# A hybrid decoder layer on one core: 384 instead of 256 tokens gathered, the choice of experts in two stages

## The reference

```python
def peer_ffn(xn, wq, k1, k2, u_tab, v_tab):       # 16384 experts, 8 heads, top 16 a head
    q = (xb @ wq).reshape(P_BLOCK, P_HEADS, 2, half)
    v1, i1 = lax.top_k(s1, P_TOPK)                # s1, s2: q against 128 keys each
    v2, i2 = lax.top_k(s2, P_TOPK)
    cand = v1[..., :, None] + v2[..., None, :]    # 256 candidates
    sc, sel = lax.top_k(cand, P_TOPK)
    gate = jax.nn.softmax(sc, axis=-1)
    hid = jnp.einsum('thkd,td->thk', u_tab[eidx], xb)
    act = jax.nn.gelu(hid) * gate
    return jnp.einsum('thk,thkd->td', act, v_tab[eidx])
```

## Time and profile before

| | |
|---|---|
| median of 3 runs | 4345.15 us (4343.4 to 4349.7) |
| profiled execution | 4344.95 us, span 4343.2 us |
| PE, PEld busy | 90%, 85% |
| DVE, ACT, POOL busy | 59%, 28%, 24% |
| granted PE clock, mean | 0.939 |
| moved | 694.92 MB, mean 160 GB/s |

### The profile page before, as it was taken

One profiled execution on the slowest core, in us unless ns is written; L12 is line 12 of the kernel. 1 busy time (PEld: TensorE's weight loads), 2 busy tenths in 40 slices (PEclk: granted clock), 3 DMA queues, 4 the chain that ended last, 5 costly groups with the idle time before them and its releaser, 6 DMA issues. The chain is left out here.

```text
span 4343.2 us, 55276 instructions
## 1 busy us (share of the span) xinstructions
PE 3913.2 (90%) x21975; PEld 3699.0 (85%) x21975; DVE 2575.6 (59%) x4489; ACT 1203.1 (28%) x1885; POOL 1049.0 (24%) x713
## 2 busy tenths in 40 slices
PE   4799875659999969999989998999979999999998
PEld 3799554538888859999989998999979999999998
DVE  3100435352222158686977775666668888888886
ACT  2111424221111122222277772222212222222221
POOL 1000100000000022222156665665522222222221
PEclk8899777569999989999999999999989999999999
DMA  2301020011111012222134448999988888878885
GB/s 97 74 30 40 8 78 20 12 36 44 44 43 68 30 47 74 80 76 79 69 148 180 178 172 319 353 349 355 348 303 278 271 276 276 270 269 271 277 278 179
DMA packets 287365, 694.92 MB, mean 160 GB/s; under 512 B 22225, under 2 KB 133505, under 8 KB 283179
## 3 DMA queue, kind: packets, MB, share of 16 engines
q1 hardware_dynamic: 193171, 367.85, 25.4%
q0 software_dynamic: 75072, 271.23, 17.7%
q10 hardware_dynamic: 18912, 53.04, 3.1%
HBM read 578.38 MB, written 114.16 MB: 159 GB/s over the span
## 5 line engine op out<-in xcount | busy, mean ns | idle before, releaser
L76 PE MATMUL ps<-x_act_high,x_v_high 128*128 128x400 f32 x2048 | 706.6, 345 | 27.6 <-DVE x_v_low L2190 27.6
L77 PE MATMUL ps<-x_act_low,x_v_high 128*128 128x400 f32 x2048 | 704.0, 344 | 0.0
L78 PE MATMUL ps<-x_act_high,x_v_low 128*128 128x400 f32 x2048 | 702.7, 343 | 0.0
L1957 POOL DMA_INDIRECT rows<-in_v,row_of x256 | 243.1, 950 | 757.8 <-DVE xn L1986 725.8
L1957 POOL DMA_INDIRECT rows<-in_u_rows,row_of x256 | 327.1, 1278 | 369.5 <-DVE row_hid L1983 313.3
L76 PEld LDWEIGHTS ps<-x_act_high,x_v_high 128*128 128x128 f32 x2048 | 385.8, 188 | 28.9 <-issue 28.9
L2199 DVE TENSOR_TENSOR xn<-xn,ps 128x400 f32<-128x400 f32 x512 | 291.5, 569 | 175.1 <-PE ps L78 175.1
L77 PEld LDWEIGHTS ps<-x_act_low,x_v_high 128*128 128x128 f32 x2048 | 385.1, 188 | 0.0
L78 PEld LDWEIGHTS ps<-x_act_high,x_v_low 128*128 128x128 f32 x2048 | 384.9, 188 | 0.1
L76 PE MATMUL ps<-hd_high,h_u_high 128*128 128x400 f32 x1024 | 353.5, 345 | 13.7 <-DVE h_u_low L2062 13.7
L77 PE MATMUL ps<-hd_low,h_u_high 128*128 128x400 f32 x1024 | 352.0, 344 | 0.0
(11 more groups left out here) (345 smaller groups left out, 8007.0 us busy)
## 6 DMA issues: line engine op xcount, KB each, us to landing
x_v_raw<-in_v SPq DMA_DIRECT2D x128, 512.0 KB, 9.6
gates<-gm_out SPq DMA_DIRECT2D x25, 2048.0 KB, 7.2
x_g<-gates SPq DMA_DIRECT2D x32, 1600.0 KB, 10.1
x_act_raw<-kept SPq DMA_DIRECT2D x128, 400.0 KB, 5.0
h_u_raw<-in_u SPq DMA_DIRECT2D x64, 512.0 KB, 6.8
kept<-h_hid ACTq DMA_DIRECT2D x64, 400.0 KB, 6.8
wq_raw<-in_u SPq DMA_DIRECT2D x40, 512.0 KB, 3.4
kept<-kept_act ACTq DMA_DIRECT2D x40, 400.0 KB, 2.4
```

What stands on the lines that cost most here:

```text
L76: pe.matmul(out, w[0], x[0], start=first, stop=False)
L77: pe.matmul(out, w[0], x[1], start=False, stop=False)
L78: return pe.matmul(out, w[1], x[0], start=False, stop=last)
L1957: pool.indirect_dma_start(m.rows[:, s % ROWS, :], None, src, bass.IndirectOffsetOnAxis(ap=m.row_of[:, t, k:k + 1], axis=0)).then_inc(r.loa ...
```

## The change

- GT becomes 3: 384 tokens are gathered (768 row jobs), 672 are dense (halves of 336 columns, 84 groups of the gate matrix).
- `choose_experts` is called twice. The first call (`rowc`) serves the three gathered tiles, with 13 table tiles (US) beside it, and computes their rows' indices. The second (`densec`) serves the other six tiles, with 94 table tiles (UD) and 21 row jobs a turn (ROWS_TURN) beside it.
- In the second call POOL's queue holds splits and gathers in one fixed order; DVE does 21 row jobs before the first pick, after each pick of even scores and after each head.
- The gate matrix has 21 table tiles beside it (BESIDE), one for each block of four groups. `finish_hidden` is gone; 13 + 94 + 21 = 128. The 411 row jobs left go to `add_outputs`.
- The rows of u run further ahead of those of v (LEAD 40 instead of 8).
- In `project` POOL waits for the tenth split piece before it writes the bias.
- `norm_and_split` turns a third tile, after the copies of the first two.

```diff
-GT = 2
+GT = 3
-EARLY = 40
-BESIDE = 24
+US = 13
+UD = 94
+BESIDE = 21
 ROWS = 6
-ROWS_BESIDE = 4
+ROWS_TURN = 21
+LEAD = 40
...
             @block.gpsimd
             def _(pool):
                 pool.wait_ge(ready, 1)
+                pool.wait_ge(low, 10)
                 pool.dma_start(d["skew"], ...
...
-def choose_experts(nc, m, d, sem):
+def choose_experts(nc, m, d, sem, c, r):
-    for n in range(2, TURNS):
-        for _ in range(2 + n % 2):
+    for n in range(1, TURNS):
+        while e < c.count_u * n // (TURNS - 1):
             turns[n].append(("u", e))
             e += 1
...
+    def upto(slot):
+
+        return c.rows * max(0, slot + 2)
...
             def _(pool):
-                for j in range(len(jobs)):
+                def split(j):
                     pool.wait_ge(w_high, j + 1)
                     pool.tensor_tensor(w[1][:, j % RING], raw[:, j % 2], w[0][:, j % RING].bitcast(F32),
                                        ALU.subtract).then_inc(w_low, 1)
+
+                split(0)
+                j = 1
+                for n, turn in enumerate(turns):
+                    a, z = upto(n - 2), upto(n - 1)
+                    for i in range(len(turn)):
+                        split(j)
+                        j += 1
+                        gather_rows(pool, m, d, r, a + (z - a) * (i + 1) // len(turn))
+                    gather_rows(pool, m, d, r, z)
...
+                def row_jobs_of(slot):
+
+                    while r.done < upto(slot):
+                        row_job(dve, m, r)
...
+                row_jobs_of(-1)
...
                 for h in range(HEADS):
                     for s in range(2):
+                        n = 2 * h + s
+                        dve.wait_ge(sc_kept, NG * (n + 1))
...
+                        if s == 0:
+                            row_jobs_of(n)
...
                     after(0)
+                    row_jobs_of(2 * h + 1)
                 dve.wait_ge(expd, HEADS)
                 gate_sums(HEADS - 1, dve, step, after)
...
+                    c = Mem()
+                    c.tag, c.h, c.chunks, c.tiles = "rowc", m.hs, [(0, TG)], list(range(GT))
+                    c.gate, c.first_u, c.count_u, c.rows = m.row_gate[:], 0, US, 0
+                    choose_experts(nc, m, d, sem, c, r)
...
+                c.tag, c.h, c.chunks, c.tiles = "densec", m.hd, HALVES, list(range(GT, NT))
+                c.e1, c.e2, c.gate, c.first_u, c.count_u, c.rows = m.e1, m.e2, m.gate, US, UD, ROWS_TURN
+                choose_experts(nc, m, d, sem, c, r)
...
                 build_gate_matrix(nc, m, d, sem)
-                r = row_sums(nc, m, sem)
-                finish_hidden(nc, m, d, sem, r)
             add_outputs(nc, m, d, sem, r)
```

More of the change, by code:

```diff
@@ L253, in _ @@
                     pe.wait_ge(scaled, k + 1)
-                    for i in range(GT):
-                        mm = pe.transpose(m.ps[:, 2 * i + k // 4, k % 4 * P:k % 4 * P + P], full[:, k, i * P:i * P + P], ident)
-                    mm.then_inc(n_turned, 1)
+                    for i in range(2):
+                        mm = turn(full, i, 2 * i, k)
+                mm.then_inc(n_turned, 1)
+                pe.wait_ge(rows_kept, 2)
+                for k in range(KT):
+                    mm = turn(m.x2, 2, 4, k)
+                mm.then_inc(x_turned, 1)
+                for k in range(KT):
+                    mm = turn(full, 2, 6, k)
+                mm.then_inc(n_turned, 1)
             @block.vector
@@ L1552, in scores @@
                     pe.wait_ge(q_kept, n + 1)
-                    for g in range(3):
-                        u = 3 * n + g
+                    for g, group in enumerate(groups):
+                        u = NG * n + g
                         if u >= 2:
                             pe.wait_ge(sc_kept, u - 1)
[L1557 to L1560, removed]
+                        for i, rows in group:
+                            mm = pe.matmul(m.ps[0:rows, 6 + u % 2, (i % 4) * NK:(i % 4) * NK + NK],
+                                           q[:, n % 2, i * P:i * P + rows], keys[:, n % 2, :], start=True, stop=True)
                         mm.then_inc(scored, 1)
@@ L1655, in _ @@
                 after(0)
[L1657 to L1672, removed]
@@ L1674, in _, with best16 @@
-                tiles = range(NT)
+                row_jobs_of(-1)
+                def best16(values, out, where):
+                    for i, rows in tiles:
+                        step(dve.max(out(i, rows, 0), values(i, rows)))
+                    for i, rows in tiles:
+                        after(nt - 1)
+                        step(dve.max_index(where(i, rows, 0), out(i, rows, 0), values(i, rows)))
+                    for i, rows in tiles:
+                        after(nt - 1)
+                        step(dve.match_replace(values(i, rows), out(i, rows, 0), values(i, rows), NEGK))
+                    for i, rows in tiles:
+                        after(nt - 1)
+                        step(dve.max(out(i, rows, 1), values(i, rows)))
+                    for i, rows in tiles:
+                        after(nt - 1)
+                        step(dve.max_index(where(i, rows, 1), out(i, rows, 1), values(i, rows)))
@@ L1687, in _ @@
+                    for i, rows in tiles:
+                        step(dve.tensor_tensor(cand[0:rows, i], top[0:rows, 0, i, :].unsqueeze(2).broadcast_to([rows, TOPK, TOPK]),
+                                               top[0:rows, 1, i, :].unsqueeze(1).broadcast_to([rows, TOPK, TOPK]), ALU.add))
                     after(0)
@@ L1766, in _ @@
                     act.copy(turned_in[s][:, a:a + r], m.ps[:, i % 8, 0:r]).then_inc(t_kept, 1)
-                act.copy(m.row_gate[:], m.gate[:, 0:GT, :])
             @block.vector
@@ L1900, in _ @@
                         gelu(n, 0)
-                for x in kept_stored:
-                    act.wait_ge(x, 16 * (BESIDE // 2))
+                n = TD // TBG
+                gelu(n - 1, 1)
+                keep(n - 1)
+                for i, x in enumerate(kept_stored):
+                    act.wait_ge(x, 16 * ((BESIDE + 1 - i) // 2))
             @block.sync
@@ L1943, in row_sums @@
     r.last_of = [None] * GT
-    r.done = 0
+    r.done = r.issued = 0
     r.loaded = [sem(f"row_loaded{i}") for i in range(ROWS)]
@@ L1947, in row_sums, with gather_rows @@
     return r
-def gather_rows(pool, m, d, r, first, upto):
-    for s in range(first, min(upto, len(r.jobs))):
+def gather_rows(pool, m, d, r, upto):
+    while r.issued < upto:
+        s = r.issued
         kind, t, k = r.jobs[s]
@@ L1959, in gather_rows @@
                                 ).then_inc(r.loaded[s % ROWS], 16)
+        r.issued += 1
 def row_gelus(act, m, r, first, upto):
@@ L1973, in row_job @@
     kind, t, k = r.jobs[s]
-    row = m.rows[:, s % ROWS, :].rearrange("p (a c) -> p a c", c=TG)
+    sums = m.n_rows[t] if kind == "u" else m.y_rows[t]
+    row = m.rows[:, s % ROWS, :].rearrange("p (a c) -> p a c", c=sums.shape[-1])
     if s in r.first_v:
```

284 lines of the change are left out of this document (115 added, 169 removed).

## The result

The changed kernel takes 4371.4 us (median of four runs) against 4344.3 for the kernel before on the same chip: a ratio of 1.0060, 95% interval 1.0043 to 1.0078. It is slower by 27 us; 42 were forecast. Its profiled execution has a span of 4370.1 us, 26.9 more than before.

The account below looks back on a forecast made before the run. PE, busy 93 to 98%, was taken to set the pace. Terms -10 + 204 + 1124 - 624 - 92 - 573 + 13 = +42 on a median of 4345.15 us gave 4387, likeliest 4345 to 4425, wider range 4265 to 4480.

Parts of the forecast that it names:

- the likeliest case: Whole kernel: the forecast of 4387 us itself, chance 0.56, with its own range of 4345 to 4425.
- Narrower tiles: Table tiles and output products: 6144 matmuls each fall by 0.0275 us apiece, 338 us of PE, if others let PE use it.
- Bias spread: Before the first choice: value piece ready at 159.5 instead of 176.5, 17 gained, 4 and 3 lost, together -10 us.
- Choice for 384: First choice of experts: PE's 174 us exceed DVE's 157; with start and last head 204 us (190 to 225).
- Choice for 672: Second choice: start 43, even turns 457, seven stalled turns 561, end 63, together 1124 us (986 to 1210).
- The held split: Second choice: POOL's fourth split queues behind a gather waiting for DVE's row; PE idles 19 us in seven turns, 138 in all.
- Splits and rows on one port: Second choice: POOL's splits and DVE's rows share a port pair and block each other; 0.6 us allowed per split.
- Rival C: Second choice, slower: splits lose the port to two rows each, 1.7 us more; +80, 4467 us; chance 0.14.
- Gate matrix: Gate matrix stage: blocks of 15.4 us, 21 of them plus 21 around make 344, 92 us less (332 to 370).
- add_outputs: Output stage: 32 groups of 35.3 us with 12.84 rows each, plus 25 to start, 1155 us, +13 (1097 to 1273).
- DMA ends last, DVE a close second: In add_outputs: DMA needs 33.8 us a group, 34.5 to 35.2 at its sustained share, DVE 33.4, PE 29.6.
- Rival D: In add_outputs, faster: DMA isn't a limit, groups take say 31.5 us; whole 4265 us; chance 0.08.

Follow-up runs that it names:

- run 5: The kernel before with only POOL's wait for the tenth weight piece put in ahead of the bias spread: 4330.9 us, ratio 0.9965.
- Run 2: Changed kernel with POOL's queue holding only six gathers before the sixth split of even turns, the rest later: 4275.1 us, ratio 0.9829.
- run 1: Changed kernel with DVE's rows of odd scores moved from behind the whole head to right behind the first picking: 4333.2 us, ratio 0.9973.
- run 3: Changed kernel with eight of the second choice's 94 table tiles moved behind the last scores: 4360.9 us, ratio 1.0037.
- run 9: Changed kernel with POOL holding at six gathers, eight table tiles in the last turn, no rows before choosing, 22 rows a slot: 4300.8 us, ratio 0.9894.
- Run 10: Changed kernel with only DVE's gate matrix subtraction for the next table tile moved one group later: 4339.8 us, ratio 0.9989.
- Run 6: Changed kernel with DVE working on 8 of a row's 1024 columns in add_outputs, all gathers kept: add_outputs 1009.6 us against 1132.4.
- run 7: Changed kernel with each add_outputs gather bringing 512 of 1024 columns, DVE working on all: add_outputs 1098.3 us against 1132.4.

## Why the prediction was right, point by point

The direction and the time were right, 4371 against 4387, within the likeliest case's own range, and the second choice, on which it hung, came out as its mechanism says. That the whole came within 16 us is in part luck: add_outputs was forecast 35 us too dear and the gate matrix 15 too cheap.

**Narrower tiles.** Right that PE saves (its matmuls of 336 columns follow each other in 0.154 us, as forecast) and that others decide how much of it counts.

**Bias spread.** Right: value piece split at 159.0 (forecast 159.5), no 22 us wait for the second piece, -9.0 for -10. By the traces 14.1 were gained (run 5, for 13) and 5.1 lost to the rest (for 3).

**Choice for 384.** Right: 207.6 for 204; PE and DVE are busy for the same 177.6 us.

**Choice for 672.** Right in total and nearly so in its parts. PE is back at pace 42 us into the stage (split from 1791.96 to 1794.63; forecast 43), seven pairs of turns last 134 to 140, 137.1 on average (57 + 80.1 = 137.3), the tail 64.2 (63). Even turns last 76.5 to 82.6 us (78 and 83). The held split cost 118.8 and not 133 of waits, 17 each instead of 19, and the granted clock of the stage is 0.91 where the old choice had 0.99. Run 2 shows that it is POOL's order. What the sum did not hold is that POOL is a bound of its own behind it: run 1 moves the wait, run 3 takes 59 us of products out of the turns and shortens them by 32, and run 9 has fewer products in its pairs than run 2 and longer pairs.

**Splits and rows on one port.** Rival C priced the split as the loser. It loses little, and the rows lose more (rows, then splits, in the second choice):

```profile
L2043 DVE CUSTOM_DVE_ANT_1 rows<-rows,xn x256: 1210/1225/4039, 1768.7 to 2855.9; 128x1024 f32<-128x1024 f32 x128
...
L2045 DVE SCALAR_TENSOR_TENSOR xn<-rows,row_hid,xn x95: 1273/1285/4089, 2298.9 to 2877.5; 128x1024 f32<-128x1024 f32 x95
...
L1602 POOL TENSOR_TENSOR densec_wq_low<-densec_wq_raw,densec_wq_high x110: 2347/2412/2802, 1758.1 to 2793.6; 128x1024 fp32r<-128x1024 f32 x110
```

The splits last 2.347 to 2.802 us. The rows of u take 1.451 on average against 1.220 in the earlier trace rows, and with those of v that adds some 75 us to DVE; what of that counts I did not measure. The Trainium skill ("SBUF — State Buffer", Who interferes with whom) has it that the order of issue decides who blocks. The trace agrees: all 53 rows above 1.4 us lie beside a split, 50 of them began after it, and they end 1.08 to 1.09 us after the split does, while the splits above 2.43 us are those that began during a row.

**Gate matrix.** Two sizes were off, in opposite directions: the wait of DVE for ScalarE's cast, for which I left 0.6 a block, is 3.1, and DVE's work, which I put at 14.8, is 13.1, so that a block takes 16.2 us in the trace instead of 15.4. Run 10 shows that without this wait the block comes down to PE's pace.

**add_outputs.** The step that failed: "DMA ends last, DVE a close second". I had taken the DMA time of a group as fixed, 33.8 us, from shares, and stretched it to the 0.96 to 0.98 that finish_hidden had shown. Run 6 moves the same bytes in 30.3 a group, at a share of 1.04, and run 7 shows DVE ending last at 32.8, against a forecast of 33.4; with 1.1 for landing a group takes 33.9 and not 35.3. Over 32 groups that is -45, of which the whole stage shows -35 (+13 to -22.2; where the other 10 are is open); the gate matrix's +15 and +6 of the smaller terms stand against it, and so +42 became +27. Rival D's premise was right; its 31.5 was not, because DVE ends last before PE's pace is reached. PE's waits there were ended not by DVE's adds, as I had expected, but by its splits of the value tiles (79.8 us in 59 waits from 3270 to 4340 us).

## What to carry to other kernels

When an in-order queue serves two consumers, look for the instruction that can stand longest and count what is behind it: here one gather, waiting for a buffer, held a split that another engine needed, and reordering the queue alone turned a loss of 27 us into a gain of 70. Taking work off the engine that seems busiest gives little where another one hands out the pieces, so after each mended wait read which engine now sets the turn. A DMA share near 1 says that transfers are always under way, not that they are what ends last: halve the bytes, or the work of the engine beside them, before calling it the bound.

## What the runs showed of the hardware

The share of DMA can pass 1: 1.04 at 383 GB/s in run 6, against 0.95 at 342 in the changed kernel. There the landing of one value tile took 18.1 us instead of 9.7, and one row's packets 0.580 x 900 / 382 = 1.37 us instead of 0.530 x 900 / 341 = 1.40, so time per byte hardly changed while landings took twice as long.

A gather that follows a split on POOL often takes 1.75 us, and later ones mostly 0.94, as at 2173.66 in the timeline above; I had priced gathers by their mean. DVE's rows make the difference. Of the 357 gathers of the second choice, the 269 that begin while DVE works on a row take up to 1.99 us (median 1.48), and the 88 others at most 1.06. In run 6, where DVE's work on a row is all but gone, the long ones are gone too (gathers from 3300 to 4200 us, in the changed kernel and then in run 6):

```profile
L2015 POOL DMA_INDIRECT rows<-in_v,row_of x227: 932/939/1865, 3299.1 to 4196.9; - x114
```

```profile
L2015 POOL DMA_INDIRECT rows<-in_v,row_of x270: 932/937/956, 3299.6 to 4199.2; - x135
```
